# Masked logits written times the negative scale, and VectorE's scaling two rows behind, in the attention stage of a streaming encoder step

## The chip, the cores and the metric

The kernel runs on one core of one Trainium2 chip. The metric is the device time of one execution in microseconds (us), as the median of several runs. The engines are named TensorE (PE, its weight loads PEld), VectorE (DVE), ScalarE (ACT), GpSimd (POOL) and SyncE (SP).

## What is computed

One inference step of a one-layer encoder: 1024 new frames of one prompt stream behind 16 meta tokens, and 16 new frames for each of 8 sample streams with 528 cached rows. There is a projection, a pooling branch, sparse attention over keys that an indexer selects, an output projection, and a mixture of 32 experts. The change touches only the softmax of the sparse attention:

```python
logits = jnp.einsum('bqgrd,bqkgd->bqgrk', qg, k_sel, preferred_element_type=jnp.float32) * ATTN_SCALE
logits = jnp.where(valid[:, :, None, None, :], logits, -jnp.inf)
p = jax.nn.softmax(logits, axis=-1)
o = jnp.einsum('bqgrk,bqkgd->bqgrd', p.astype(v_sel.dtype), v_sel)
```

The kernel does not gather keys. It computes the logits over all admissible keys and adds a bias of -1e30 to those that are not selected.

## The kernel before

Each engine has its own instruction list in the order in which the code is written; an engine runs its list strictly in order and waits on semaphores. Nothing is scheduled by a compiler, so the order of the loops below is the order on the chip.

The attention stage lies between about 598 and 826 us. The prompt's 1024 queries are 8 tiles of 128, each with 2 groups of key heads: 16 groups, `PG`, from the longest (1040 keys) to the shortest (144 keys). A group has `REP` = 4 rows of probabilities (query heads), each a tile of 128 queries by `n_keys` keys. The 8 sample streams are one row of 544 keys each and are put between the groups from step 6 on (`S_STEP`). A row is cut into one, two or three parts of at most 512 keys (`chunks_of`): three for the first two groups, two for the next eight and for the samples, and one for the last six groups (400, 272 and 144 keys).

In step `st` TensorE transposes the probabilities of group `st` (L1081), multiplies them with the values (L1099, the last tile L1095), and between these takes the logits of group `st + 1` (three matmuls each, L1054, L1057, L1060) into three PSUM banks in turn. From step 7 on it then does the transposes (L1108, L1112) and the values (L1124) of the sample row of the step before, and the logits of the next sample (L1066, L1070).

A row goes through these functions:

- `ttr` on VectorE, called a take below (L1942): it adds the bias to a part of the logits, writes the sum to SBUF and keeps the part's maximum. In the trace one call is two instructions, CUSTOM_DVE_ANT_0 and the read of its accumulator. With more than one part a reduce over the maxima follows (L1947), and in every case a one-column multiply by the negative scale, which gives the exponential's offset (L1951). `link` makes the next instruction wait for the one in front of it.
- `expo` on ScalarE (L1572): the exponential of the row with that offset, which also gives the row's sum. It waits for `a_max`, counted by L1951.
- `scale` on VectorE: the reciprocal of the sum (L1955) and the multiplication of the row by it (L1957). It waits for `a_exp`, counted by the exponential.
- `tevac` on ScalarE: copies of the transposed probabilities out of PSUM (L1585, for the last tile of a group L1582, for a sample row L1587 and L1589).

VectorE's list for a step is in the loop over `STEPS`: for each of the four rows the take, and behind it the scaling of the row before (behind row 0's take that of the sample row). Then come the scaling of the last row, then the rest of the next queries (`q_rest`, L1982), the evacuation of the heads (`oevac`, L1971 and L1972), and then the take of the next sample row. The first group's takes and scalings are a loop of their own ahead of that. ScalarE's list for a step is fixed likewise: the copy of each transposed tile, with the exponentials of rows whose logits TensorE took one tile before, and the sample's exponential at the very end of the step.

The rest of the kernel starts from the stage's end: TensorE's output projection waits for all heads (`a_oe`), and so do SyncE's loads for it.

Of the kernel before, what the change touches and what calls it, by code (L numbers as in the profile page):

```python
# [24 lines left out]
ALU = mybir.AluOpType  # L25
ACT = mybir.ActivationFunctionType
AX = mybir.AxisListType
# [15 lines left out]
HEADS, KVH, HD, REP = 8, 2, 128, 4  # L43
# [5 lines left out]
ATTN_SCALE = HD ** -0.5  # L49
# [9 lines left out]
MASKED = -3.0e38  # L59
# [12 lines left out]
def splits(n, most=512):  # L72

    k = -(-n // most)
    w = -(-n // (2 * k)) * 2
    return [(c, min(c + w, n)) for c in range(0, n, w)]


def build(nc, a):
    ctx = ExitStack()  # L80
    with ctx:
# [145 lines left out]
        mx3 = sm(8, 3)  # L227
        mx1 = sm(8)
        nmx = sm(8)
# [264 lines left out]
        PG = [("p", i, g) for i in reversed(range(NPT)) for g in range(KVH)]  # L494
        NPG = len(PG)
        NG_ALL = NPG + DEC_B
        S_STEP = {6 + b: ("s", b, 0) for b in range(DEC_B)}
        STEPS = range(-1, NPG)

        QO, PO = [], []  # L500
# [5 lines left out]
        def heads_of(x):  # L506
            return REP if x[0] == "p" else 1

        def chunks_of(x):
            return splits(n_keys[x[1]]) if x[0] == "p" else splits(SK)  # L510
# [5 lines left out]
        S_AT = {x: sum(heads_of(y) * len(chunks_of(y)) for y in QO[:n]) for n, x in enumerate(QO)}  # L516
        T_AT = {x: sum(trs_of(y) for y in PO[:n]) for n, x in enumerate(PO)}
        O_AT = {x: n for n, x in enumerate(PO)}
        KEY_CHUNKS = splits(SAMPLE0)

        def high_at(n):
# [31 lines left out]
        def stat(x, r, kind):  # L553

            if x[0] == "p":
                q = 4 * slot_of(x) + r
                return {"max3": mx3[:, q, :], "max": mx1[:, q:q + 1], "neg": nmx[:, q:q + 1],
                        "sum": rsum[:, q:q + 1], "inv": rinv[:, q:q + 1]}[kind]
            q = 8 * slot_of(x)
            o, w = {"max3": (0, 3), "max": (3, 1), "neg": (4, 1), "sum": (5, 1), "inv": (6, 1)}[kind]  # L560
            return RS[:, q + o:q + o + w]

        def plan(st):
# [64 lines left out]
        a_sm = sem("logits_taken")  # L628
# [738 lines left out]
        def _(act):  # L1367
# [198 lines left out]
                act.wait_ge(pool_out[s], 128)  # L1566

            def expo(x, r):
                uu = U_AT[x] + r
                act.wait_ge(a_max, uu + 1)  # L1570
                p = probs_of(x, r)[:, 0:chunks_of(x)[-1][1]]
                nc.scalar.activation(p, p, ACT.Exp, bias=stat(x, r, "neg"), scale=ATTN_SCALE,  # L1572
                                     accum_out=stat(x, r, "sum")).then_inc(a_exp, 1)

            def tevac(x, j):
# [225 lines left out]
        def _(dve):  # L1801
# [5 lines left out]
            def link(ins):  # L1807

                dve_n[0] += 1
                ins.then_inc(dve_c, 1)  # L1810
                dve.wait_ge(dve_c, dve_n[0])
# [119 lines left out]

            def ttr(x, r):
                kind, i, g = x
                uu = U_AT[x] + r
                ch = chunks_of(x)
                if r == 0 and before(x):
                    dve.wait_ge(a_t, T_AT[before(x)] + trs_of(before(x)))
                for m, (c0, c1) in enumerate(ch):
                    n = S_AT[x] + r * len(ch) + m
                    dve.wait_ge(a_s, n + 1)  # L1940
                    add = sc[i][:, c0:c1] if kind == "p" else zero[:, 0:c1 - c0]
                    nc.vector.tensor_tensor_reduce(out=probs_of(x, r)[:, c0:c1], in0=logits_bank(x, n)[:, 0:c1 - c0], in1=add,  # L1942
                                                   scale=1.0, scalar=MASKED, op0=ALU.add, op1=ALU.max,
                                                   accum_out=stat(x, r, "max3")[:, m:m + 1]).then_inc(a_sm, 1)
                dve.wait_ge(a_sm, n + 1)
                if len(ch) > 1:
                    link(nc.vector.tensor_reduce(stat(x, r, "max"), stat(x, r, "max3")[:, 0:len(ch)], AX.X, ALU.max))  # L1947
                    src = stat(x, r, "max")
                else:
                    src = stat(x, r, "max3")[:, 0:1]  # L1950
                ts(stat(x, r, "neg"), src, -ATTN_SCALE, None, ALU.mult).then_inc(a_max, 1)  # L1951

            def scale(x, r):
                dve.wait_ge(a_exp, U_AT[x] + r + 1)
                link(nc.vector.reciprocal(stat(x, r, "inv"), stat(x, r, "sum")))  # L1955
                p = probs_of(x, r)[:, 0:chunks_of(x)[-1][1]]
                ts(p, p, stat(x, r, "inv"), None, ALU.mult).then_inc(a_p, 1)  # L1957
# [41 lines left out]
            for st in STEPS[1:]:  # L1999
                if st + 1 < NPG:  # L2000
                    for r in range(REP):
                        ttr(PG[st + 1], r)
                        if r >= 1:
                            scale(PG[st + 1], r - 1)
                        elif st - 1 in S_STEP:
                            scale(S_STEP[st - 1], 0)
                    scale(PG[st + 1], REP - 1)
                if st < NPG - 2:
                    q_rest(PG[st + 2])
                if st >= 0:  # L2010
                    oevac(PG[st])
                if st - 1 in S_STEP:
                    oevac(S_STEP[st - 1])
                if st in S_STEP:
                    ttr(S_STEP[st], 0)
# [575 lines left out]
```

## Time and profile before

| | |
|---|---|
| median of 3 runs | 1324.01 us (1324.01 to 1324.23) |
| the profiled execution, its own time | 1322.85 us |
| its span, first to last instruction | 1321.1 us |
| mean granted TensorE clock | 0.986 |
| TensorE busy (matmuls) | 1259.8 us, 95% of the span |
| VectorE busy | 931.8 us, 71% |
| ScalarE busy | 500.7 us, 38% |
| GpSimd busy | 463.8 us, 35% |

Busy time is a sum over the whole span. The ends of matmuls are modelled in such a profile, so TensorE's share overstates how near it is to its peak. A share says nothing of a single stage; for that the stretches below are read.

### The profile page before, as it was taken

To read this page: it belongs to the slowest core of one execution; us is meant where nothing else is said; L and a number is where in the kernel's file an instruction comes from. 1 tells how busy PE (TensorE), PEld (TensorE's weight loads), DVE (VectorE), ACT (ScalarE), POOL (GpSimd) and SP (SyncE) were. 2 spreads that over 40 slices of the span, in tenths; PEclk is the share of its full clock that TensorE was granted. 3 is DMA by queue.
4 is the path that set the end of the run, shared out by engine and by line. 5 is a ranking of instruction groups with operands and counts; after the bars stand their busy time and mean duration, and the time that the engine had idled before them with its cause. 6 is when DMAs were issued, how large, how long until landed. Compare 5 with 4: busy or idle time off the path is not lost.

```text
span 1321.1 us, 21407 instructions
## 1 busy us (share of the span) xinstructions
PE 1259.8 (95%) x7551; PEld 1097.6 (83%) x7551; DVE 931.8 (71%) x2249; ACT 500.7 (38%) x1090; POOL 463.8 (35%) x752
## 2 busy tenths in 40 slices
PE   6999999999989999998999998999999979999996
PEld 6999999999979999998777766999788858777752
DVE  5665888888989989864677766232566568776647
ACT  6554222122212112324665644000423247655644
POOL 5801595968884215654000000220011143333320
PEclk9999999999999999998999999999999989999999
DMA  7201232121213321103000220935220258999849
GB/s 264 72 26 43 78 86 82 37 80 38 71 36 109 95 86 51 34 1 101 1 1 17 68 73 29 328 128 183 113 80 33 96 213 304 355 344 336 317 159 394
DMA packets 79458, 163.85 MB, mean 124 GB/s; under 512 B 12418, under 2 KB 48082, under 8 KB 78210
## 3 DMA queue, kind: packets, MB, share of 16 engines
q1 hardware_dynamic: 64977, 128.84, 28.7%
q0 software_dynamic: 12656, 27.62, 6.3%
q10 hardware_dynamic: 1728, 6.10, 1.1%
q8 instruction: 61, 1.00, 0.3%
q14 instruction: 36, 0.29, 0.1%
HBM read 137.86 MB, written 39.21 MB: 134 GB/s over the span
## 4 chain that ended last, share of the span: by engine, by line
PE 74%; DMA 10%; POOL 5%; DVE 4%; ACT 3%; issue 2%; SPq 1%; POOLq 0%; ACTq 0%; DVEq 0%
PE bank L887 11%; PE bank L888 11%; PE bank L889 11%; PE bank L1099 4%; DMA region_w<-in_wd 4%; PE bank L1174 3%; PE bank L1168 3%; PE bank L1017 2%; PE bank L1081 2%; PE bank L1185 2%; PE bank L1186 2%; PE bank L1187 2%; PE bank L1293 2%; DMA region_h<-in_wd 2%; DMA region_q<-in_wd 2%; PE bank L1170 2%
## 5 line engine op out<-in xcount | busy, mean ns | idle before, releaser
L1900 DVE MAX8 small<-region_kv 128x8 f32<-128x272 f32 (+4 forms) x241 | 190.2, 828 | 47.6 <-DVE region_kv L1905 47.5
L887 PE MATMUL bank<-h_hi,w_hi 128*128 128x384 f32 (+1 forms) x576 | 196.2, 341 | 0.0
L888 PE MATMUL bank<-h_lo,w_hi 128*128 128x384 f32 (+1 forms) x576 | 196.1, 341 | 0.0
L1905 DVE MATCH_REPLACE8 region_kv<-small,region_kv 128x272 f32<-128x272 f32 (+4 forms) x241 | 195.5, 819 | 0.0
L889 PE MATMUL bank<-h_hi,w_lo 128*128 128x384 f32 (+1 forms) x576 | 194.5, 338 | 0.0
L2253 POOL TENSOR_TENSOR w_lo<-w_stage,w_hi 128x512 fp32r<-128x512 f32 x64 | 80.8, 1296 | 144.8 <-ACT w_hi L1397 144.7
L887 PE MATMUL bank<-w_hi,h_hi 128*128 128x256 f32 x448 | 128.9, 288 | 2.3 <-ACT region_q L1460 2.3
L889 PE MATMUL bank<-w_hi,h_lo 128*128 128x256 f32 x448 | 126.0, 281 | 0.0
L888 PE MATMUL bank<-w_lo,h_hi 128*128 128x256 f32 x448 | 125.9, 281 | 0.0
L889 PEld LDWEIGHTS bank<-h_hi,w_lo 128*128 128x128 f32 x576 | 108.8, 189 | 0.0
L888 PEld LDWEIGHTS bank<-h_lo,w_hi 128*128 128x128 f32 x576 | 108.2, 188 | 0.6
L887 PEld LDWEIGHTS bank<-h_hi,w_hi 128*128 128x128 f32 x576 | 108.0, 188 | 0.5
L887 PEld LDWEIGHTS bank<-w_hi,h_hi 128*128 128x128 f32 x448 | 84.2, 188 | 2.6 <-ACT region_q L1460 2.5
L889 PEld LDWEIGHTS bank<-w_hi,h_lo 128*128 128x128 f32 x448 | 84.5, 189 | 0.0
L888 PEld LDWEIGHTS bank<-w_lo,h_hi 128*128 128x128 f32 x448 | 84.4, 188 | 0.0
L1556 ACT ACTIVATE region_q<-bank 128x384 f32<-128x384 f32 x48 | 23.6, 492 | 159.6 <-PE bank L889 159.6
L2459 POOL DMA_INDIRECT expert_rows_scratch<-region_t,small_i x32 | 35.7, 1116 | 119.4 <-ACT region_t L1740 100.7
L1099 PE MATMUL bank<-region_t,region_kv 128*128 128x512 f32 (+1 forms) x144 | 73.1, 598 | 0.3 <-issue 0.3
L1174 PE MATMUL bank<-o_hi,wao_lo 128*128 128x384 f32 x192 | 68.6, 357 | 0.0
L1168 PE MATMUL bank<-o_hi,wao_hi 128*128 128x384 f32 x192 | 65.6, 342 | 1.5 <-DVE o_lo_prompt L1972 1.5
L1308 PE MATMUL bank<-expert_high,rowsT_hi 128*128 128x256 f32 x256 | 64.9, 292 | 1.5 <-ACT rowsT_hi L1733 1.5
L2026 DVE TENSOR_TENSOR region_t<-bank,region_t 128x384 f32<-128x384 f32 x24 | 13.4, 558 | 73.3 <-PE bank L1174 62.7
(345 smaller groups left out, 3153.1 us busy)
## 6 DMA issues: line engine op xcount, KB each, us to landing
w_stage<-in_w_in SPq DMA_DIRECT2D x72, 256.0 KB, 3.4
region_kv<-in_xa SPq DMA_DIRECT2D x16, 512.0 KB, 5.5
region_q<-in_wg SPq DMA_DIRECT2D x12, 512.0 KB, 6.6
region_q<-in_wu SPq DMA_DIRECT2D x12, 512.0 KB, 19.6
region_q<-in_wd SPq DMA_DIRECT2D x12, 512.0 KB, 23.3
region_w<-in_wg SPq DMA_DIRECT2D x10, 512.0 KB, 6.9
region_w<-in_wu SPq DMA_DIRECT2D x10, 512.0 KB, 20.2
region_w<-in_wd SPq DMA_DIRECT2D x10, 512.0 KB, 23.2
```

Source lines behind the costliest of these rows:

```text
L887: mm(out, st_hi(k), mv_hi(k), start=(k == 0), stop=False)
L888: mm(out, st_hi(k), mv_lo(k), start=False, stop=False)
L889: last = mm(out, st_lo(k), mv_hi(k), start=False, stop=(k == KD - 1))
L1017: last = mm(b[:, 0:384], wpool[:, g % 2, k, cc * P:(cc + 1) * P], dT[:, k, c0:c1], start=(k == 0), stop=(k == 1))
L1099: mm(out[:, :], values[0:rows, :], PT[0:rows, t % 3, :], start=(j == 0), stop=False, skip_group_check=True)
L1168: mm(out, hi, o_hi[:, k, c0:c1], start=(k == 0), stop=False, skip_group_check=True)
L1174: last = mm(out, lo, o_hi[:, k, c0:c1], start=False, stop=(k == KD - 1), skip_group_check=True)
L1308: mm(out, rowsT_hi[:, par, k, :], high[:, :, k, :], start=(k == 0), stop=False, skip_group_check=True)
L1900: nc.vector.max(m8[:, q, :], x).then_inc(dve_c, 1)
L1905: nc.vector.match_replace(x, m8[:, q, :], x, TAKEN).then_inc(dve_c, 1)
L2253: tt(w_lo(n)[:, kk * m:kk * (m + 1), :], stage(s if s < KD else s % 4, kk, wd), w_hi(n)[:, kk * m:kk * (m + 1), :].bitcast(F32), ALU.subtr ...
L2459: pool.indirect_dma_start(out=y_d, out_offset=bass.IndirectOffsetOnAxis(ap=idx, axis=0), in_=src, in_offset=None, bounds_check=2 * TOK - 1 ...
```

## The change

The take now multiplies the biased logits by the negative scale while it writes them, and keeps the minimum in place of the maximum. The minimum is the exponential's offset as it stands, and the exponential's own scale is -1. The one-column multiply and the link ahead of it go. A row of one part has no instruction between take and exponential; its exponential waits for `a_sm`, which counts takes. A row of more parts keeps the reduce, which now counts `a_max`. Besides, in the loop over the steps VectorE scales a row two takes later and not one; the loop of the first group keeps its order.

```diff
+        IN_PARTS = [(x, r) for x in QO for r in range(heads_of(x)) if len(chunks_of(x)) > 1]
...
             def expo(x, r):
-                uu = U_AT[x] + r
-                act.wait_ge(a_max, uu + 1)
+                if len(chunks_of(x)) > 1:
+                    act.wait_ge(a_max, IN_PARTS.index((x, r)) + 1)
+                else:
+                    act.wait_ge(a_sm, S_AT[x] + r + 1)
                 p = probs_of(x, r)[:, 0:chunks_of(x)[-1][1]]
-                nc.scalar.activation(p, p, ACT.Exp, bias=stat(x, r, "neg"), scale=ATTN_SCALE,
+                nc.scalar.activation(p, p, ACT.Exp, bias=stat(x, r, "least"), scale=-1.0,
                                      accum_out=stat(x, r, "sum")).then_inc(a_exp, 1)
...
                     nc.vector.tensor_tensor_reduce(out=probs_of(x, r)[:, c0:c1], in0=logits_bank(x, n)[:, 0:c1 - c0], in1=add,
-                                                   scale=1.0, scalar=MASKED, op0=ALU.add, op1=ALU.max,
-                                                   accum_out=stat(x, r, "max3")[:, m:m + 1]).then_inc(a_sm, 1)
-                dve.wait_ge(a_sm, n + 1)
+                                                   scale=-ATTN_SCALE, scalar=-MASKED, op0=ALU.add, op1=ALU.min,
+                                                   accum_out=stat(x, r, "least3")[:, m:m + 1]).then_inc(a_sm, 1)
                 if len(ch) > 1:
-                    link(nc.vector.tensor_reduce(stat(x, r, "max"), stat(x, r, "max3")[:, 0:len(ch)], AX.X, ALU.max))
-                    src = stat(x, r, "max")
-                else:
-                    src = stat(x, r, "max3")[:, 0:1]
-                ts(stat(x, r, "neg"), src, -ATTN_SCALE, None, ALU.mult).then_inc(a_max, 1)
+                    dve.wait_ge(a_sm, n + 1)
+                    nc.vector.tensor_reduce(stat(x, r, "least"), stat(x, r, "least3")[:, 0:len(ch)], AX.X,
+                                            ALU.min).then_inc(a_max, 1)
...
                     for r in range(REP):
                         ttr(PG[st + 1], r)
-                        if r >= 1:
-                            scale(PG[st + 1], r - 1)
-                        elif st - 1 in S_STEP:
+                        if r >= 2:
+                            scale(PG[st + 1], r - 2)
+                        elif r == 0 and st - 1 in S_STEP:
                             scale(S_STEP[st - 1], 0)
-                    scale(PG[st + 1], REP - 1)
+                    for r in (REP - 2, REP - 1):
+                        scale(PG[st + 1], r)
```

On VectorE a late step looks as follows, here the one whose prompt rows have 272 keys, from the reduce of a sample row's maxima on. A take is the pair of ISA rows, a scaling is RECIPROCAL and the TENSOR_SCALAR behind it. Before:

```order
L1947 TENSOR_REDUCE region_s<-region_s 128x1 [waits logits_taken]
L1951 TENSOR_SCALAR region_s<-region_s 128x1 [waits dve_chain]
L1942 ISA region_t,small<-bank,region_kv 128x272 [waits logits_done,probs_transposed]
L1942 ISA small 128x1
L1951 TENSOR_SCALAR small<-small 128x1 [waits logits_taken]
L1955 RECIPROCAL region_s<-region_s 128x1 [waits exp_done]
L1957 TENSOR_SCALAR nbuf<-nbuf,region_s 128x544 [waits dve_chain]
L1942 ISA region_t,small<-bank,region_kv 128x272 [waits logits_done]
L1942 ISA small 128x1
L1951 TENSOR_SCALAR small<-small 128x1 [waits logits_taken]
L1955 RECIPROCAL small<-small 128x1 [waits exp_done]
L1957 TENSOR_SCALAR region_t<-region_t,small 128x272 [waits dve_chain]
```

And in the changed kernel, from the same reduce on:

```order
L1949 TENSOR_REDUCE region_s<-region_s 128x1 [waits logits_taken]
L1944 ISA region_t,small<-bank,region_kv 128x272 [waits logits_done,probs_transposed]
L1944 ISA small 128x1
L1954 RECIPROCAL region_s<-region_s 128x1 [waits exp_done]
L1956 TENSOR_SCALAR nbuf<-nbuf,region_s 128x544 [waits dve_chain]
L1944 ISA region_t,small<-bank,region_kv 128x272 [waits logits_done]
L1944 ISA small 128x1
L1944 ISA region_t,small<-bank,region_kv 128x272 [waits logits_done]
L1944 ISA small 128x1
L1954 RECIPROCAL small<-small 128x1 [waits exp_done]
L1956 TENSOR_SCALAR region_t<-region_t,small 128x272 [waits dve_chain]
L1944 ISA region_t,small<-bank,region_kv 128x272 [waits logits_done]
```

The one-column multiplies are gone, and the take of row 2 stands ahead of the scaling of row 0.

ScalarE's list in the same step keeps its order; what the exponentials of the prompt rows wait for is another semaphore. Before:

```order
L1572 ACTIVATE nbuf,region_s<-nbuf,region_s 128x544 [waits max_ready]
L1585 COPY region_t<-bank 80x512 [waits probs_transposed]
L1601 CAST queries_hi<-region_q 128x512 [waits logits_done]
L1585 COPY region_t<-bank 128x512 [waits probs_transposed]
L1572 ACTIVATE region_t,small<-region_t,small 128x272 [waits max_ready] x2
```

After:

```order
L1575 ACTIVATE nbuf,region_s<-nbuf,region_s 128x544 [waits max_ready]
L1588 COPY region_t<-bank 80x512 [waits probs_transposed]
L1604 CAST queries_hi<-region_q 128x512 [waits logits_done]
L1588 COPY region_t<-bank 128x512 [waits probs_transposed]
L1575 ACTIVATE region_t,small<-region_t,small 128x272 [waits logits_taken] x2
```

The sample row has two parts, so its exponential still waits for `max_ready`, now counted by the reduce; the prompt rows wait for `logits_taken`, counted by the take.

## Rows read from the trace of the kernel before

**Rows 1.** Stretches: us, busy PE PEld DVE ACT POOL, granted clock, DMA.
```profile
640.00:656.00 16.00, 16.00 (x79) 11.18 (x78) 12.15 (x37) 9.74 (x18) 0.00 (x0) 1.00 0.00 0
789.00:800.00 11.00, 9.35 (x65) 6.76 (x64) 7.89 (x33) 5.44 (x16) 2.76 (x3) 1.00 0.33 101
```

**Rows 2.** TensorE's waits, 754 to 820 us: total us, times, longest.
```profile
PE bank L1124 <- ACT region_t L1589: 4.1, 3, 1.7
PE bank L1112 <- ACT nbuf L1582: 1.3, 2, 0.9
PE bank L1108 <- DVE nbuf L1957: 0.3, 1, 0.3
PE bank L1108 <- ACT region_t L1585: 0.2, 1, 0.2
```

**Rows 3.** ScalarE's waits for VectorE, 754 to 820 us.
```profile
ACT region_t L1572 <- DVE small L1951: 3.8, 11, 0.5
```

**Rows 4.** VectorE in time: start, duration, instruction, idle before it and releaser.
```profile
792.61 0.15 DVE L1947 TENSOR_REDUCE region_s<-region_s 128x1 f32<-128x2 f32 x1
792.80 0.15 DVE L1951 TENSOR_SCALAR region_s<-region_s 128x1 f32<-128x1 f32 x1
...
795.85 0.16 DVE L1955 RECIPROCAL small<-small 128x1 f32<-128x1 f32 x1 [0.74 <-ACT region_t L1572]
...
796.33 0.43 DVE L1942 CUSTOM_DVE_ANT_0 region_t<-bank,region_kv 128x272 f32<-128x272 f32 x1
...
796.80 0.15 DVE L1951 TENSOR_SCALAR small<-small 128x1 f32<-128x1 f32 x1
796.87 0.15 DVE L1955 RECIPROCAL small<-small 128x1 f32<-128x1 f32 x1
```

**Rows 5.** ScalarE in time, the same step.
```profile
792.99 0.75 ACT L1572 ACTIVATE nbuf<-nbuf,region_s 128x544 f32<-128x544 f32 x1 [5.03 <-DVE region_s L1951]
...
795.62 0.20 ACT L1572 ACTIVATION_READ_ACCUMULATOR region_t<-region_t,small 128x1 f32 x1
795.71 0.52 ACT L1572 ACTIVATE region_t<-region_t,small 128x272 f32<-128x272 f32 x1
...
796.99 0.52 ACT L1572 ACTIVATE region_t<-region_t,small 128x272 f32<-128x272 f32 x1 [0.41 <-DVE small L1951]
...
798.01 0.52 ACT L1572 ACTIVATE region_t<-region_t,small 128x272 f32<-128x272 f32 x1 [0.40 <-DVE small L1951]
```

**Rows 6.** TensorE in time, its waits in four of the late steps.
```profile
775.85 0.28 PE L1112 MATMUL bank<-consts,nbuf 128*32 128x128 f32 x1 [0.91 <-ACT nbuf L1582]
...
799.38 2.42 PE L1124 MATMUL bank<-region_t,region_h 128*128 128x64 f32 x20 [1.66 <-ACT region_t L1589]
...
810.05 2.42 PE L1124 MATMUL bank<-region_t,region_h 128*128 128x64 f32 x20 [1.09 <-ACT region_t L1589]
...
819.98 2.42 PE L1124 MATMUL bank<-region_t,region_h 128*128 128x64 f32 x20 [1.33 <-ACT region_t L1589]
```

**Rows 7.** VectorE and TensorE in time at the start of the stage.
```profile
615.15 0.15 DVE L1951 TENSOR_SCALAR small<-small 128x1 f32<-128x1 f32 x1
...
618.20 0.15 DVE L1951 TENSOR_SCALAR small<-small 128x1 f32<-128x1 f32 x1
...
620.78 1.05 PE L1081 MATMUL bank<-consts,region_w 128*80 128x128 f32 x4 [2.94 <-DVE region_w L1957]
```

**Rows 8.** An early step's last scaling, and TensorE's last values of it.
```profile
653.22 0.70 DVE L1957 TENSOR_SCALAR region_t<-region_t,small 128x912 f32<-128x912 f32 x1
...
657.93 0.38 PE L1095 MATMUL bank<-nbuf,region_kv 128*128 128x256 f32 x1
```

**Rows 9.** Fused reduces: count, ns min/median/max, first and last start, shapes.
```profile
L2084 DVE CUSTOM_DVE_ANT_0 region_s<-nbuf,region_s x18: 192/193/194, 971.7 to 1073.0; 128x32 f32<-128x32 f32 x18
...
L1942 DVE CUSTOM_DVE_ANT_0 nbuf<-bank,region_h x12: 441/442/443, 753.5 to 814.1; 128x272 f32<-128x272 f32 x12
```

**Rows 10.** A stretch after the stage's end; the granted clock is the third figure from the right.
```profile
827.00:830.00 3.00, 3.00 (x11) 3.00 (x10) 0.00 (x0) 0.00 (x0) 0.00 (x0) 0.50 0.70 196
```

More of the change, by code:

```diff
@@ L556, in stat @@
                 q = 4 * slot_of(x) + r
-                return {"max3": mx3[:, q, :], "max": mx1[:, q:q + 1], "neg": nmx[:, q:q + 1],
+                return {"least3": mx3[:, q, :], "least": mx1[:, q:q + 1] if len(chunks_of(x)) > 1 else mx3[:, q, 0:1],
                         "sum": rsum[:, q:q + 1], "inv": rinv[:, q:q + 1]}[kind]
             q = 8 * slot_of(x)
-            o, w = {"max3": (0, 3), "max": (3, 1), "neg": (4, 1), "sum": (5, 1), "inv": (6, 1)}[kind]
+            o, w = {"least3": (0, 3), "least": (3, 1), "sum": (5, 1), "inv": (6, 1)}[kind]
             return RS[:, q + o:q + o + w]
@@ L1933, in ttr @@
                 kind, i, g = x
-                uu = U_AT[x] + r
                 ch = chunks_of(x)
```

## The prediction, made before the changed kernel ran

> **What bounds the kernel now.** Read the stretches of the attention stage first [rows 1]: the reader is to see that in a typical early step (640 to 656 us) TensorE is busy all 16.00 of 16.00 us at the full clock, while VectorE has 12.15 and ScalarE 9.74. Nothing that makes VectorE faster can shorten such a step. Late in the stage (789 to 800 us) TensorE has 9.35 of 11.00 us: there something else sets the pace. So next read who waits, on TensorE, from 754 to 820 us [rows 2]: 4.1 + 1.3 + 0.3 + 0.2 = 5.9 us, nearly all for ScalarE's copies of transposed probabilities out of PSUM (L1589, L1582). These six steps (the sample values of each, L1124, begin at 763, 777, 788, 799, 810 and 820 us) are where the change can pay; 5.9 us is the ceiling of that part as the list has it. Then read what ScalarE waits for in the same stretch [rows 3]: the prompt rows' exponentials wait 3.8 us in 11 waits, all for L1951, the small multiply that the change removes. Last, one step in order of time, VectorE [rows 4], ScalarE [rows 5] and TensorE [rows 6].
>
> In that step (792.6 to 799.4 us) the chain is: VectorE takes the sample logits, reduces (792.61) and multiplies (792.80); ScalarE starts the sample exponential at 792.99, then goes through its in-order list of copies and exponentials without a pause until the exponential of row 2 (796.99, idle 0.41) and of row 3 (798.01, idle 0.40), then come two more copies, and TensorE starts the sample values at 799.38 after 1.66 us idle. Why are rows 2 and 3 late? VectorE's reciprocal of row 0 sat idle 0.74 us until ScalarE finished row 0's exponential (795.85), and the take of row 2's logits (796.33) stands behind it in VectorE's queue. That take shows no wait for TensorE: the logits were there.
>
> **The change, part by part.** (a) *The small multiply is gone* for all 72 rows of probabilities (64 prompt, 8 sample), and with it one link. From the start of the multiply to the start of the exponential is 792.99 - 792.80 = 0.19 us [rows 4, 5]; this is what every exponential gains whose chain was on the path. Without the multiply a two-part row ends at the reduce, which starts where it did (792.61), and a one-part row ends at the take itself. In each of the six late steps the sample exponential starts 0.19 us earlier and ScalarE's whole list moves with it: 6 x 0.19 = 1.1 us.
>
> (b) *The scaling two rows behind.* The take of row 2 no longer waits behind row 0's scaling. VectorE was free at 795.85 - 0.74 = 795.1 us, so the take that began at 796.33 can begin at about 795.0 and be done more than 0.8 us before ScalarE's turn (796.99 - 0.41 less the lead of 0.19). Row 3's take then stands behind row 0's scaling. That can start 0.19 us earlier than 795.85, at 795.66; reciprocal and scaling are 796.33 - 795.85 = 0.48 us, and from the start of a take to that of the multiply behind it 796.80 - 796.33 = 0.47: ready at 796.6, while ScalarE, with row 2's exponential at 796.3 and 0.5 us for it, comes to row 3 at 796.8. Both idles of ScalarE go. An idle in the list understates the gap, since an instruction that need not wait starts before the one ahead of it has ended: row 1's exponential at 795.71 starts 0.11 us before the end of the accumulator read ahead of it (795.62 + 0.20) [rows 5]. So I add 0.1 us per wait: 3.8 + 11 x 0.1 = 4.9 us over the 11 waits [rows 3].
>
> (a) and (b) together shorten ScalarE's list by 6.0 us over six steps, but TensorE can only take what it waits for, step by step. At 799.38 it is 0.19 + 0.51 + 0.50 = 1.2 of 1.66, so 0.45 stay; at 810.05 a step of average waits (0.19 + 2 x 0.45 = 1.1) covers all of 1.09; at 819.98 1.1 of 1.33 + 0.33 (the second is the wait for the scaled sample row, L1957), so 0.55 stay; at 775.85 all of 0.91 and at the two steps left all of theirs [rows 2, 6]. That is 5.9 - 0.45 - 0.55 = 4.9 us. Matmul ends are modelled, and where a matmul starts a tenth or two after its predecessor's usual spacing the list shows no wait; three of the six steps have such places, and I add 0.3 for them.
>
> (c) *The start of the stage.* The first group's scores are taken while the last projections run. Two multiplies stand in series there [rows 7]: the one at 615.15 delays VectorE's scaling and the take behind it, which TensorE's next logits wait for, and the one at 618.20 delays the last exponential; TensorE idles 2.94 us before L1081 at 620.78. GpSimd's rest of the keys, which the next logits want, is behind a ScalarE copy that is behind this exponential, so it moves too. 2 x 0.19 = 0.4 us.
>
> (d) *Costs.* The last scaling of a step now has two others directly before it, after the last take. In the early steps I get it 0.2 us later than at present. It ends at 653.22 + 0.70 = 653.92 us, and TensorE asks for it only after the last values of the step, whose matmul is at 657.93 [rows 8]: 4 us of cover. In the late steps it is no later than now, since the exponentials are earlier. Behind the scalings VectorE holds the rest of the queries and the evacuation of heads, wanted later still. The probability buffers, the three logits banks and ScalarE's order do not change, and banks come free sooner. The price without that cover would be 0.2 us in each of nine steps, 1.8 us.
>
> (e) *The take itself* has another factor and takes a minimum. No row shows that form. The nearest are another fused reduce of the same family (multiply, add) at 192 ns for 32 columns and the present one at 442 ns for 272 [rows 9]: (442 - 192) / 240 = 1.04 ns per column across two members. I take the same price; the far bound, twice per column, is 0.28 us more for a 272-column take.
>
> A rule of the Trainium skill bears on the price in (a). On the row, 192 ns start to start is paid from multiply to exponential, and the reciprocal that needs nothing from the multiply follows it after 796.87 - 796.80 = 0.07 us [rows 4]. The Trainium skill (VectorE: DVE Perf Modes, section on the DRAIN you can't avoid) says that the pipe is emptied between two operations with or without a semaphore, so that only the number of operations counts. By that rule each of the eight steps of the chain would give the 0.15 us of the operation and not 0.19, and the sum would be 0.3 us smaller; the trace does not agree for these one-column operations.
>
> **The sum.** 4.9 + 0.3 + 0.4 = 5.6 us. Everything behind the stage hangs on its end (loads for the next stage are issued when the last head is evacuated), so it shifts as a whole. The profiled execution took 1322.85 us with a span of 1321.1, and would become 1317.2; the median of the runs is 1324.01, 1.2 us above it, and I take the same difference: 1324.0 - 5.6 = 1318.4 us.
>
> **The rivals.** *Only the short chain pays.* If row 2's and row 3's takes were held by something other than the scaling (TensorE's logits, a bank), (b) would give nothing and the gain is 1.1 + 0.4 = 1.5 us: 1322.5. For it: the late steps are short and everything in them is tight. Against it: the take at 796.33 shows no wait of its own [rows 4]. 0.11. *Part of it comes back.* TensorE has waits of its own in these steps that now end last (a transpose that ScalarE's copy must follow): half of (b), 3 to 4.5 us, about 1320.2. 0.13.
>
> *The clock adds to it.* TensorE's granted clock is 0.50 (1.2 GHz, not 2.4) from 827 to 830 us [rows 10], after the idle of the late steps and of the last evacuation. 3 us at half the rate cost 1.5 us. Denser late steps could avoid this, 1316.9; a low stretch elsewhere could as well grow. 0.13 for the better side. The Trainium skill (TensorE: Matmul & The Clock Gate, Part 1) calls the number of slow matmuls variable from run to run, which would put this within the spread of executions rather than on the change.
>
> *The other side: the new take is dearer.* In an early step VectorE has 12.15 us of work in 16 [rows 1]; four rows of 912 columns at 1.04 ns are 3.8 us of it, and 4 x 0.15 go with the multiplies. At k times the price per column VectorE has 11.5 + 3.8 (k - 1) us. At k = 2 that is 15.3, still under 16, and the late steps lose 0.28 where they gain about 0.9, so the kernel is still faster. It tips at k of about 2.3; at 3 it is 19.1 us, 3 us over in each of eight steps, or some 20 us more in all: 1344. Nothing in the two rows of the family speaks for it. 0.05.
>
> **How the numbers follow.** My forecast (4.9 to 6.3 us gained, 1317.7 to 1319.1) has 0.58, the clock rival 0.13, the part that comes back 0.13, the short chain only 0.11, the dearer take 0.05. The range from 1316.2 to 1321.0 takes in the first three. A measurement of this kernel tells a difference from none at about 0.2%, 2.6 us; the third case lies on the faster side of it, the fourth within it. Faster 0.84, no change 0.11, slower 0.05.
>
> **What would show it.** Right: no one-column multiply between take and exponential; in the late steps row 2's take directly behind row 1's, ScalarE's waits before the prompt exponentials nearly gone, TensorE's wait for L1124 down from 4.1 to about 1 us, the early steps unchanged to a tenth, the start of the stage 0.4 us shorter. Wrong: takes of 272 columns clearly above 442 ns, a TensorE wait for VectorE's scaling at the head of a step, or a new ScalarE wait for TensorE's transposes.

## The result, and the profile after

The changed kernel takes 1314.39 us (median of 6 runs, 1311.57 to 1316.64), the kernel before 1323.1 us beside it (6 runs, 1321.36 to 1324.23). The ratio is 0.9935, 95% interval 0.9924 to 0.9946: 8.6 us less, 7.0 to 10.1. I had forecast 1318.4 us and 1316.2 at the lowest. The direction was right; the time lies below the range.

The profiled execution took 1313.87 us (span 1312.1, mean granted clock 0.986; TensorE busy 1254.2 us, VectorE 921.0, ScalarE 499.4, GpSimd 463.8). Line numbers shift by -1 to +3 with the edit: L1124 is now L1125, the take L1942 is L1944, the reduce L1947 is L1949, the reciprocal L1955 is L1954, the scaling L1957 is L1956, the exponential L1572 is L1575, the copies L1585 to L1589 are L1588 to L1592.

Stretches of the profile after; columns as in [rows 1]:

```profile
640.00:656.00 16.00, 16.00 (x78) 11.17 (x78) 10.33 (x32) 9.62 (x18) 0.00 (x0) 1.00 0.00 1
783.00:794.00 11.00, 10.56 (x73) 7.82 (x73) 7.97 (x29) 5.26 (x17) 2.78 (x3) 1.00 0.32 101
824.00:830.00 6.00, 6.00 (x41) 6.00 (x40) 1.95 (x4) 1.05 (x1) 4.71 (x2) 1.00 1.10 357
```

The early steps are as full as they were: VectorE fell from 12.15 to 10.33 us in 16, TensorE is at 16.00 both times. A late step has TensorE at 10.56 of 11 where it was 9.35. And the stage ends without the half clock that stood at 827 to 830 us [rows 10].

TensorE's waits, 740 to 830 us of the profile after (to be held against [rows 2]):

```profile
PE bank L1169 <- DVE o_lo_prompt L1971: 1.5, 1, 1.5
PE bank L1125 <- ACT region_t L1592: 1.0, 3, 0.4
```

The 4.1 us ahead of the sample values are 1.0, and the waits for the transposes are gone. The first line is the end of the stage, outside [rows 2]'s window; it was 1.5 us before too. ScalarE's waits in these steps (753 to 812 us), against 3.8 us in 11 in [rows 3]:

```profile
ACT nbuf L1575 <- DVE region_s L1949: 24.2, 5, 4.8
ACT region_t L1592 <- PE bank L1113: 0.7, 2, 0.4
ACT region_t L1590 <- PE bank L1109: 0.7, 1, 0.7
```

No exponential of a prompt row (`region_t`) waits any more. What is left is the sample exponential at the head of the list, which waits for its reduce from the step's end; ScalarE's own waits for TensorE's transposes were 0.9 us in 2 before and are 1.4 us in 3. One late step on VectorE, then on ScalarE (rows as in [rows 4] and [rows 5]):

```profile
787.69 0.16 DVE L1949 TENSOR_REDUCE region_s<-region_s 128x1 f32<-128x2 f32 x1
788.25 0.44 DVE L1944 CUSTOM_DVE_ANT_0 region_t<-bank,region_kv 128x272 f32<-128x272 f32 x1 [0.40 <-PE bank L1061]
...
789.38 0.43 DVE L1944 CUSTOM_DVE_ANT_0 region_t<-bank,region_kv 128x272 f32<-128x272 f32 x1
...
789.74 0.44 DVE L1944 CUSTOM_DVE_ANT_0 region_t<-bank,region_kv 128x272 f32<-128x272 f32 x1
...
790.74 0.16 DVE L1954 RECIPROCAL small<-small 128x1 f32<-128x1 f32 x1 [0.56 <-ACT region_t L1575]
```

```profile
787.88 0.75 ACT L1575 ACTIVATE nbuf<-nbuf,region_s 128x544 f32<-128x544 f32 x1 [4.84 <-DVE region_s L1949]
...
790.61 0.51 ACT L1575 ACTIVATE region_t<-region_t,small 128x272 f32<-128x272 f32 x1
```

Row 2's take (789.74) stands directly behind row 1's (789.38), and only then does the reciprocal of row 0 sit idle for its exponential. From reduce to exponential it is now 787.88 - 787.69 = 0.19 us; it was 792.99 - 792.61 = 0.38.

TensorE's sample values of the last three steps, and the first transposes of the stage (against [rows 6] and [rows 7]):

```profile
793.25 2.42 PE L1125 MATMUL bank<-region_t,region_h 128*128 128x64 f32 x20 [0.43 <-ACT region_t L1592]
802.88 2.42 PE L1125 MATMUL bank<-region_t,region_h 128*128 128x64 f32 x20 [0.24 <-ACT region_t L1592]
811.62 2.42 PE L1125 MATMUL bank<-region_t,region_h 128*128 128x64 f32 x20 [0.33 <-ACT region_t L1592]
...
619.56 0.83 PE L1082 MATMUL bank<-consts,region_w 128*80 128x128 f32 x3 [2.75 <-DVE region_w L1956]
```

**Where the time came from, execution against execution.** The spans differ by 9.0 us. I take the start of the same instruction in both traces. The changed kernel is 0.8 us ahead already at 111 us, before anything that was edited. At the first transposes it is 1.2 ahead (620.78 to 619.56), so the start gave 0.4. At the first sample values it is 2.8 ahead (736.52 to 733.74): both clocks fell to half in the idle at the start, but before it lasted 10.2 us (618.6 to 628.9), after 6.8 (617.8 to 624.7), of which TensorE was idle the first 1.7. This 1.6 us belongs to the execution and not to the change: from the stage's first logits to the first sample values the kernel before took 139.0 us, this profile of the changed kernel 137.0, and a second profile of the same changed kernel (e10 below) 138.6. From the second sample values to the last it is 69.79 us before and 64.19 after: 5.6 us. At the first matmul of the output projection the lead is 8.4, at its last 10.0, since the low stretch at 827 to 830 us is missing after. At 1271 us it is 10.3, at the end 9.0: the tail, from the last expert rows' transfers on, took 1.3 us more.

So the chains gave 0.4 + 5.6 = 6.0 us, where I had 5.6. The rest is clock, and what differs between any two executions. The experiments are about which of the two.

### The profile page after: what moved, and what is told of

Its sections match the earlier page's. It is cut to its first block, busy times and chain, and to the rows that moved or that the text cites. A ratio compares the mean times of both kernels' runs of the same rounds, so it can differ in the third digit from the quotient of the medians.

```text
span 1312.1 us, 21335 instructions
## 1 busy us (share of the span) xinstructions
PE 1254.2 (96%) x7551; PEld 1093.2 (83%) x7551; DVE 921.0 (70%) x2177; ACT 499.4 (38%) x1090; POOL 463.8 (35%) x752
## 4 chain that ended last, share of the span: by engine, by line
PE 77%; DMA 9%; POOL 6%; ACT 3%; DVE 2%; SPq 1%; issue 1%; POOLq 0%; ACTq 0%; DVEq 0%
PE bank L889 11%; PE bank L888 11%; PE bank L890 11%; DMA region_w<-in_wd 5%; PE bank L1100 4%; PE bank L1175 3%; PE bank L1082 3%; PE bank L1169 3%; PE bank L1018 3%; PE bank L1186 2%; PE bank L1187 2%; PE bank L1188 2%; PE bank L1294 2%; DMA region_q<-in_wd 2%; PE bank L1171 2%; PE bank L1125 1%
```

## The experiments

All were timed beside the kernel before, e1 to e4 in one session, e5 to e8, e9 to e12 and e13 to e16 in one each. Every session had another chip, and the medians of the kernel before were 1322.65, 1322.05, 1322.45 and 1323.39 us in them, so a difference across sessions carries about a microsecond that is not the kernels'. A filler is a matmul of a constant tile into a PSUM bank that is overwritten before it is read; it changes no result.

### The two halves of the change

e1_multiply_only is the changed kernel with the scaling order of before:

```diff
-                        if r >= 2:
-                            scale(PG[st + 1], r - 2)
-                        elif r == 0 and st - 1 in S_STEP:
+                        if r >= 1:
+                            scale(PG[st + 1], r - 1)
+                        elif st - 1 in S_STEP:
```

> Only the small multiply is gone; VectorE scales one row behind, as in the kernel before. Own theory (chains in the six late steps and at the start, by the rows): each late step gains 0.19 us at the sample exponential, 0.19 at the exponential of row 2 and up to 0.2 at that of row 3, where TensorE waits for it: from the sample values of the seventh step to those of the last 69.8 us (before) become about 66.8; the start of the stage gains 0.4. Together 3.2 to 3.5 us, plus what the clock gives or takes (0 to 3 us). Rival (what is beyond the 6.0 us of the chains comes from the early steps, where VectorE is less busy): the eight early steps are shorter too, by some tenths each. Second rival (only the scaling order counts): 1.1 us or less in the late steps.

e2_two_behind_only is the kernel before with the reverse of that edit.

> Only the scaling is two rows behind; the small multiply stays. Own theory: ScalarE's waits before the exponentials of rows 2 and 3 go (about 0.9 us per late step where TensorE waits that long), the sample exponential starts as before: the late stretch of 69.8 us becomes about 65.4 (4.4 us gained), the start of the stage unchanged. The two parts alone then give 3.0 + 4.4 us against 5.6 together in this stretch, since the exponentials of rows 2 and 3 can be early only once. Rival (each part has its own gain and they add): 5.6 - 3.0 = 2.6 us here.

Measured: e1 1319.52 us (11 runs), ratio 0.9972 (0.9963 to 0.9982), which is 3.7 us less by the ratio (3.1 by the medians). e2 1315.31 (5 runs), ratio 0.9947 (0.9934 to 0.9960), 7.0 us less. TensorE's waits for the sample values in e1, then in e2 (753 to 822 us):

```profile
PE bank L1125 <- ACT region_t L1592: 2.6, 3, 1.1
```

```profile
PE bank L1124 <- ACT region_t L1589: 1.7, 3, 0.8
```

Each half takes off part of the 4.1 us, and either alone leaves more than both together (1.0). From the second sample values to the last e2 took 65.48 us, as expected (65.4), a gain of 4.3; the scaling order is the larger half, as the prediction's (b) has it. Together they give 5.6 and not the sum of 3.2 (e1, measured below with the clock held) and 4.3, since they shorten the same wait.

What did not fit is the whole time. e1 gained its chains (3.6 us), e2 gained 2.7 us more than its own. Two stretches of e1's profile, where TensorE was in the late steps (clock: third figure from the right):

```profile
796.00:804.00 8.00, 8.00 (x55) 5.79 (x56) 4.42 (x16) 2.17 (x5) 0.00 (x0) 0.79 0.00 0
816.00:824.00 8.00, 6.35 (x32) 4.76 (x32) 3.17 (x8) 1.41 (x4) 0.00 (x0) 0.79 0.00 0
```

e1, which still waits 2.6 us for the sample values, has low clock twice within the late steps. Nothing of the kind stands in e2's profile or in that of the changed kernel.

### Fillers at the wrong place

e3_before_filled and e4_after_filled are the kernel before and the changed one with a filler ahead of the wait for the last evacuations, and three at the start of the stage behind all of its waits:

```diff
             pe.wait_ge(selected, NT)
+            for i in range(3):
+                mm(bank[3][:, :], ident, consts[:, 0:512], start=True, stop=True)
...
+            pe.wait_ge(a_sm, S_AT[QO[-1]] + heads_of(QO[-1]) * len(chunks_of(QO[-1])))
+            mm(bank[2][:, :], ident, consts[:, 0:512], start=True, stop=True)
             pe.wait_ge(a_oe, NG_ALL)
```

> The kernel before with four idle matmuls of TensorE that nothing reads: three of 0.86 us in the 2.9 us of idle at the stage's start, one in the 1.5 us ahead of the output projection. Clock theory (what the change gained beyond 6.0 us is TensorE's granted clock at these two places, which depends on where the idle falls): the granted clock stays at 1.00 from 616 to 630 and from 824 to 831 us, where it was 0.50 for 10 and for 3 us, and the kernel is 4 to 6 us faster than before, 1317 to 1319. Rival (the clock follows something else, or the idle matmuls delay the work): the low stretches stay, and the time is the same or up to 1 us more.

> The changed kernel with the same four idle matmuls. Clock theory: both low stretches gone here too, so that the difference to the filled kernel before is the chains' own 6.0 us (5.5 to 6.5) and not the 8.6 us of the medians; 1311 to 1313. Its spread from execution to execution is below that of the changed kernel (5 us). Rival (the chains are worth more than the rows say, the clock nothing): the difference of the two filled kernels is again 8 to 9 us.

Measured: 1322.52 us (ratio 0.9998, 0.9989 to 1.0007) and 1318.22 (0.9958, 0.9943 to 0.9974). Both missed what the clock theory expected (1317 to 1319 and 1311 to 1313); the two are 4.3 us apart by the medians where it had 5.5 to 6.5, and e4's executions spread over 5.9 us and not under 5. In e3 the fillers at the start ran only when the wait was over, from 620.6 us on and for the most part at half clock, and pushed the stage's first transposes back from 620.8 to 624.7 us. So the pair says nothing on the start. The one at the end did its work: in e3 the stretch at 827 us is at full clock.

### The end alone, and the start at its right place

e5_before_end_filled is the kernel before with only the end filler. In e6_before_filled_early and e7_after_filled_early (the changed kernel) the ones at the start stand ahead of the waits:

```diff
-            pe.wait_ge(tr_evac, len(ROPED))
             pe.wait_ge(pj_evac, NU)
+            for i in range(6):
+                mm(bank[3][:, 0:256], ident, consts[:, 0:256], start=True, stop=True)
+            pe.wait_ge(tr_evac, len(ROPED))
             pe.wait_ge(selected, NT)
```

> The kernel before, with one 512-column filler matmul in front of the wait for the last evacuations, so that TensorE isn't idle between the attention stage and the output projection (its result is never read). Clock theory: the low stretch that the kernel before shows at 827 to 830 us goes, its out-projection stage (826.6 to 1074.4 us) gets 1.6 to 2.1 us shorter, and the median falls by as much, to about 1321. Rival (the low stretch only moves, or the rest of the time gives it back): median within 0.5 us of the kernel before.

> The kernel before, with the filler at the end and six 256-column fillers in the 2.9 us idle at the start of the attention stage, this time ahead of the waits for the first logits' probabilities. Clock theory: no low stretch at 617 to 629 us (10.2 us of it at half clock before) nor at 827 to 830, 3 to 5 us less than the kernel before, 1318 to 1320. Rival (filler doesn't keep the clock, or the stage's start is bound by VectorE and ScalarE): within 1 us of it.

> The changed kernel with the same fillers. Clock theory of the 2.6 us that my sum lacked: with both kernels filled, the difference between this and e6_before_filled_early is only what the chains give, 5.6 to 6.0 us. Rival (the 2.6 us come from elsewhere): it stays 8 to 9 us.

Measured: e5 1320.02 us, 2.0 less than before (ratio 0.9984, 0.9973 to 0.9995). Its profile has no low stretch at 827 us, and from the first matmul of the output projection to the last projection behind it (L1168 to L1232) it takes 245.5 us where the kernel before took 247.9. e7 1313.71 (0.9939, 0.9924 to 0.9955). But e6 took 1323.55 (1.0007, 0.9997 to 1.0018), no less than before, and the difference between e6 and e7 is 9.8 us: both of my expectations on e6 fell. Its profile shows why. The start is full now (the first sample values come 136.7 us after the stage's first logits, against 139.0), but the late steps have these:

```profile
800.00:804.00 4.00, 4.00 (x21) 2.06 (x21) 1.82 (x9) 0.42 (x1) 0.00 (x0) 0.60 0.01 2
820.00:824.00 4.00, 4.00 (x23) 3.82 (x22) 0.95 (x3) 0.18 (x1) 0.00 (x0) 0.53 0.00 0
```

From its first sample values to the output projection it took 94.2 us, the kernel before 90.1. These low stretches come behind the waits of 1.66 and 1.34 us for the sample values (797.5 and 819.3 us), which the change shortens; behind the one of 1.01 us between them none came. I had looked for the clock at the ends of the stage; it can sit in the late steps as well. It needn't: e5's late steps have the same waits (1.66, 1.09 and 1.33 us) without a filler in them, and e3's nearly so (1.66, 1.08 and 1.34), and in their profiles these steps are at full clock. e5:

```profile
796.00:804.00 8.00, 6.34 (x45) 4.28 (x44) 6.28 (x24) 2.17 (x8) 0.00 (x0) 1.00 0.00 1
816.00:824.00 8.00, 6.06 (x40) 4.63 (x40) 4.89 (x22) 3.65 (x13) 0.00 (x0) 1.00 0.00 0
```

Each profile is one execution, so the waits are something that half clock may follow, not something that it always follows.

### All of TensorE's idles filled

e9_before_late_filled is e5, e12_before_all_filled is e6, each with fillers in the sample values' waits as well:

```diff
+                if i >= 5:
+                    for _ in range(2):
+                        mm(ob[:, 0:256], ident, consts[:, 0:256], start=True, stop=True)
                 pe.wait_ge(a_te, t + 2)
```

> The kernel before with the end filler, and two 256-column fillers in front of the sample values' wait for the copied probabilities in the last three steps (where it waits 1.66, 1.09 and 1.33 us), so that the waits stay and TensorE isn't idle in them. Clock theory: no low stretch from 735 to 830 us in the profile, none in most executions, chains unchanged (750 to 820 us still 69.8 us); median about 1319 to 1319.5, 2.5 to 3 us less than the kernel before and a narrower spread than with the end filler alone. Rival (the 2.6 us that my sum lacked aren't the clock's): no faster than e5_before_end_filled, 1320 or more.

> e6_before_filled_early with the late fillers of e9_before_late_filled too. Its profile showed two low stretches, at 800 and 820 us. Clock theory: both go, 737 to 829 us gets 4 us shorter, and against e7_after_filled_early (1313.71) the difference falls from 9.8 us to 5.5 to 7. Rival: it stays above 8.5 us.

> The changed kernel once more, as the control for its neighbours here. Clock theory: no low stretch between 735 and 830 us in this profile either; median 1314 to 1315. With e9_before_late_filled the difference should be nearer to the 6.0 us of the chains than the 8.6 us of the first comparison: 5 to 6 us. Rival: 7.5 us or more.

Measured: e12 1320.09 us (9 runs, 1319.26 to 1320.66; ratio 0.9979, 0.9969 to 0.9988). Against e6, which ran in the session before, that is 3.5 us (3.7 by the ratios) for matmuls whose results nobody reads, and its profile has the same place at full clock:

```profile
800.00:804.00 4.00, 4.00 (x34) 3.06 (x31) 2.96 (x15) 1.92 (x5) 0.00 (x0) 1.00 0.01 2
820.00:824.00 4.00, 3.33 (x15) 1.73 (x13) 1.75 (x4) 0.85 (x2) 0.00 (x0) 1.00 0.00 0
```

Against e7 it is 6.4 us, in the range of the clock theory, but across two sessions (5.3 by the ratios). e9 missed: 1321.93 (0.9994, 0.9985 to 1.0003), no better than e5, as its rival had it. Its profile is clean from 735 to 900 us, as expected, but has half clock at the start for 10.2 us, like the kernel before; what its other executions did isn't shown. e10, the changed kernel again, took 1315.82 (0.9948, 0.9935 to 0.9961), 6.9 us less than before by the ratio, and 6.1 less than e9: just outside the 5 to 6 us that the clock theory expected, and its median is above the expected 1314 to 1315.

Then the two halves, filled, with both ends of the scale in one session. e13_multiply_filled is e1 with the fillers (one for each late wait), e14_two_behind_filled is e2 with those at start and end, e15 is e12 and e16 is e7 again.

> The kernel of e1_multiply_only with the fillers at the start, in the last three steps (one of 256 columns each) and at the end. Clock theory: with the clock held its gain over e15_before_filled_control is what its chains give, 3.2 us in the late steps and 0.4 at the start: 3.6 us, between 3.2 and 4.2. Rival: the parts' gains are no more tied to the chains than without fillers, off by over 1 us.

> The kernel of e2_two_behind_only with the fillers at the start and at the end. Clock theory: 4.3 us less than e15_before_filled_control, between 3.8 and 4.9; its surplus of 2.7 us over its chain in the first comparison is gone. Rival (the surplus is no matter of the clock): 6.5 to 7 us less.

> The kernel of e12_before_all_filled again, as the control: 1320.1 within 0.6 us, a spread under 2 us, and no low stretch between 617 and 830 us.

> The kernel of e7_after_filled_early again, beside its control on the same chip. Clock theory: 6.0 us less than e15_before_filled_control, between 5.4 and 6.6. Rival: 8 us or more.

Measured, with the lead over e15, beside the chains' gain and the gain that the same edit showed without fillers:

| filled kernel | median, us | less than e15 | chains | without fillers |
|---|---|---|---|---|
| e15, before | 1320.10 (1318.87 to 1320.76) | | | |
| e13, multiply only | 1316.38 (1315.22 to 1316.53) | 3.7 | 3.6 | 3.7 |
| e14, two behind only | 1316.00 (1314.67 to 1317.19) | 4.1 | 4.3 | 7.0 |
| e16, both | 1313.85 (1312.89 to 1315.61) | 6.25 | 6.0 | 8.6 and 6.9 |

The last column is from the ratios to the kernel before. All four expectations of the clock theory were met by the medians, and the surplus of e2 is gone. By the means the leads over e15 are 3.9, 4.0 and 5.7 us, each uncertain by 0.7 to 1.2 us (two standard errors): enough to tell e14 from 7.0 and e16 from 8 us, not to check the chains to a tenth. The profiles agree step for step: from the first sample values to the output projection e15 takes 89.9 us, e13 86.7, e14 85.8 and e16 84.5, with full clock in all four. Only e14 kept some low clock at the stage's start (0.66 from 624 to 628 us). The kernel before took 1323.39 us beside these four: filling its idles alone gives it 3.3 us. The changed kernel took 1314.39 and 1315.82 without fillers, 1313.71 and 1313.85 with them: it gains 0.5 to 2.1 us.

### A better version

After the change TensorE still waits 1.0 us for L1592. e8_after_upper_earlier casts the next queries ahead of the sample exponential, in ScalarE's idle of 4.84 us:

```diff
-                    if j == max(nb - 3, 1) and st + 2 < NPG:
+                    if j == max(nb - 3, 1) and st + 2 < NPG and st - 1 not in S_STEP:
                         q_upper(PG[st + 2])
...
                 if st in S_STEP:
+                    if st + 3 < NPG:
+                        q_upper(PG[st + 3])
                     expo(S_STEP[st], 0)
```

> The changed kernel with ScalarE's cast of the next queries (0.5 us, L1604) moved in the late steps from between the copies to the idle time of 4.84 us ahead of the sample exponential. The waits of the sample values for L1592 (1.0 us in 3) end on ScalarE's list of exponentials and copies, which gets 0.5 us shorter: they go, 0.8 to 1.0 us less, 1313.5. Rival (TensorE then waits on VectorE's scaling instead, since the last transposed tile needs it): no more than 0.3 us.

e11_after_filled_upper is this with e7's fillers.

> The changed kernel with the fillers of e7_after_filled_early and the earlier cast of e8_after_upper_earlier. The profiles gave 0.8 us at the start of the stage by the fillers, 0.9 us in the late steps by the cast: 1312.5 to 1313, 1.5 us less than e10_after_again. Rival (the tail of the kernel, which waits on transfers, takes it back): within 0.5 us of it.

Measured: e8 1314.69 us (0.9943, 0.9928 to 0.9957). In its profile the wait is 0.3 us and the way from the first sample values to the output projection 83.5 us, 1.0 shorter than the changed kernel's 84.5; in the whole time that can't be told from the changed kernel. e11 took 1312.54 (1311.32 to 1313.93; ratio to before 0.9923, 0.9910 to 0.9936), 3.3 us less than the changed kernel in the same session where I expected 1.5. It is the fastest version of all.

## Why the prediction missed, point by point

**The bound and the ceiling** held: early steps unchanged, the whole chain gain from the six late steps and the start.

**(a) and (b), the chains.** The mechanism was right in each link. A link gave 0.19 us, as the row had it. The Trainium skill (VectorE: DVE Perf Modes, The DRAIN you can't avoid) would have had only the operation's own time count; 0.38 to 0.19 us from reduce to exponential doesn't agree, though the difference is 0.04 us. I said that 0.45, 0 and 0.55 us would stay at the last three sample values; 0.43, 0.24 and 0.33 stayed. The late steps gave 5.6 us and not 5.2: the waits in the list fell as predicted, so the term of 0.3 us for stalls that the list doesn't show was too small; it was about 0.7 (5.6 less the 4.9 us of waits that the list lost). Of the signs of being wrong one stirred: ScalarE's waits for transposes grew by 0.5 us, and TensorE didn't wait longer for it.

**(c) The start** gave 0.4 us, as predicted. **(d) The costs** were nothing: the last scaling of an early step ends at 651.36 us where the lead of 2.7 us alone would have it at 651.2, and the last values are at 655.28. **(e) The take** kept its price:

```profile
L1944 DVE CUSTOM_DVE_ANT_0 nbuf<-bank,region_h x16: 429/442/444, 722.7 to 806.9; 128x272 f32<-128x272 f32 x16
```

The median is 442 ns, as in [rows 9].

**The step that failed** is the rival "the clock adds to it". I took the half clock of [rows 10] as one stretch worth 1.5 us that might go or come back elsewhere, at 0.13, and left it out of the sum. What the runs show in its place: half clock can follow each of several waits, and not only one, and the change shortens most of them. Five kernels have late waits with no filler in them (the kernel before, e1, e3, e5, e6). In their profiles e1 and e6 have two low stretches each between 795 and 830 us, the kernel before has one behind the last evacuations, and e3 and e5, which have a filler at that end, have none. Where the late waits are filled (e9, e12, e13, e15) there is none either. With the waits for the sample values at 0.8 us or less, in the changed kernel and all that scale two rows behind, there was none from 640 to 900 us in any of nine profiles (the changed kernel twice, e2, e4, e7, e8, e11, e14, e16). That the waits raise how often the clock falls is shown by the times (e2 against e14, e6 against e12); how often, in how many executions, is not, and e9 against e5 doesn't show it. A sum that shortens TensorE's idle in a stretch that already ends at half clock has to carry the clock's term with the chain's.

**How much was that?** The 1318.4 us were 4.0 too high: 0.9 of it is the base (I took 1324.0, the kernel before had 1323.1 beside the changed one), 0.4 the chains, 2.7 is left (2.6 by the ratio). Over all sessions the means are 1322.63 us for the kernel before (84 runs) and 1315.25 for the changed kernel (12 runs), 7.4 apart; filled they are 1320.0 (16 runs) and 1314.1 (11 runs), 5.9 apart. So the clock is worth about 1.5 us of it, and the rest is which executions the first series drew. The size is uncertain by about 1.4 us either way (two standard errors), since the changed kernel's 12 executions spread over 7.5 us. The mean granted clock goes the same way: 0.9855 before, 0.9873 after, and 0.990 for both once filled. It gives an estimate of its own: over 206 executions, each held against the mean of its own kernel, one whose clock was lower by 0.001 took 0.6 us longer (correlation -0.6), so 0.0018 is 1.0 us. The draw alone doesn't explain the miss: the second series of the changed kernel (1315.82) lies below my range too.

The sentence with which I left the clock out was drawn from the Trainium skill (TensorE: Matmul & The Clock Gate, Part 1), that the number of slow matmuls varies from run to run. The trace agrees that it varies (executions of the kernel before spread over 6.4 us, filled over 1.9), but a quantity that varies can still have its mean moved by the change. The same page (A second HAM failure mode: psum-queue depth-cycling) says that frequent short idles between groups of matmuls can throttle it too; e6 against e12 agrees, 3.5 us.

**Open.** Why the late fillers gave nothing without those at the start (e9 is 1.9 us slower than e5), and 3.5 us with them (e12 against e6), and why fillers at the start beside the one at the end made the kernel before slower (e6 is 3.5 us slower than e5), isn't settled. Whether half clock early in the stage changes the odds of half clock later was not tested. Each kernel has one profile, and the executions in it with several low stretches can't be looked at.

## What to carry to other kernels

When a change removes waits of the engine that sets the pace, look whether its clock is low in or just behind that stretch. If it is, the gain may be the wait and part of the low stretch: here 6.0 us of chains and some 1 to 1.5 of clock. Add it, and widen the range on that side. To split the two, fill the waits with matmuls into a bank that is about to be overwritten, ahead of the semaphore wait: if the difference between two kernels shrinks to that of their chains, the rest was the clock. Fill all the waits: some fillers without the others made this kernel slower (e6).

When VectorE's list takes rows in and finishes rows from another engine in turn, let the finishing trail by two: a take must not stand behind a reciprocal whose exponential isn't done. This gave more (4.3 us) than the deleted instruction (3.2 us).

## What was not expected of the hardware

In e6 half clock stood behind waits of no more than 1.66 and 1.34 us, in steps of some 10 us (0.60 and 0.53 over 4 us each), and in e5 the same waits had none. Matmuls that compute nothing made the kernel before 2.4 us (e12) and 3.3 us (e15) faster by the medians, with a spread of its executions of 1.4 and 1.9 us instead of 4.3 and 4.6 us of the unfilled one in the same sessions, which had more executions (21 and 11 beside 9 and 7). And the same fillers a few instructions too late, behind the wait and not ahead of it, started the stage's transposes 3.9 us later (e3), though the first sample values came no later (736.4 us, before 736.5), and gave nothing in the whole.
